# Order of three token tiles at the end of a hybrid decoder step

## The reference, cut to what matters

```python
x2 = LN2(alpha*x1 + HMoE(x1))   # top-1 group of experts, then top-2 experts in it
x3 = LN3(alpha*x2 + sigmoid(x2 @ w_ple_gate + b) * (p @ w_ple))
```

## Time and profile before

| what | value |
|---|---|
| median of three runs | 596.12 us |
| the profiled execution | 592.34 us |
| its span, first to last event | 590.7 us |
| TensorE busy | 535.6 us (91%) |
| VectorE busy | 293.3 us (50%) |
| ScalarE busy | 193.0 us (33%) |
| GpSimd busy | 58.0 us (10%) |

### The profile page before, as it was taken

The page is one execution under the profiler, slowest core; times in us unless marked ns, Lnnn a source line. Parts: engine busy times, 40 slices in busy tenths (PEclk is TensorE's granted clock), DMA queues, the critical chain, the costliest instruction groups (busy, mean ns, idle before and its releaser), DMA issues.

```text
span 590.7 us, 9533 instructions
## 1 busy us (share of the span) xinstructions
PE 535.6 (91%) x3628; PEld 385.0 (65%) x3628; DVE 293.3 (50%) x621; ACT 193.0 (33%) x363; POOL 58.0 (10%) x86
## 2 busy tenths in 40 slices
PE   4999789998999979999999999998888899888990
PEld 3999678887999978767664445444444445356870
DVE  3533786654475766686722322222222222378877
ACT  4444534443363360163141111111111121362532
POOL 2000003321352520000000000000000000000121
PEclk9999989999999999968999999999999999979996
DMA  8996237755232950195739999999999999940001
GB/s 277 370 348 216 88 117 210 252 199 165 81 131 58 326 206 1 50 426 236 275 135 423 421 421 424 420 424 421 423 420 424 419 424 417 363 184 1 1 36 53
DMA packets 47563, 151.86 MB, mean 257 GB/s; under 512 B 3104, under 2 KB 27877, under 8 KB 35104
## 3 DMA queue, kind: packets, MB, share of 16 engines
q1 hardware_dynamic: 42754, 136.93, 60.1%
q0 software_dynamic: 3728, 12.08, 6.4%
q10 hardware_dynamic: 1046, 2.37, 1.2%
HBM read 148.59 MB, written 2.90 MB: 256 GB/s over the span
## 4 chain that ended last, share of the span: by engine, by line
PE 72%; DMA 13%; DVE 9%; ACT 3%; issue 2%; SPq 0%; DVEq 0%; POOL 0%; POOLq 0%
PE bank L1482 16%; PE bank L1801 15%; DMA ring<-in_w_up_dram 11%; PE bank L1450 9%; PE bank L1814 7%; PE bank L1670 5%; PE bank L1823 2%; PE bank L1900 2%; PE bank L1748 2%; PE bank L1428 2%; PE bank L1537 1%; PE bank L1712 1%; PE bank L1702 1%; DMA arena<-in_x_prompt_dram 1%; PE bank L1807 1%
## 5 line engine op out<-in xcount | busy, mean ns | idle before, releaser
L1801 PE MATMUL bank<-ring,arena 128*64 128x256 f32 x1024 | 128.9, 392 | 10.6 <-DMA ring<-in_w_up_dram 7.3
L1801 PEld LDWEIGHTS bank<-ring,arena 128*64 128x64 f32 x1024 | 71.1, 134 | 66.6 <-issue 28.8
L1242 DVE TENSOR_TENSOR arena<-bank,arena 128x512 f32 x32 | 22.1, 692 | 143.7 <-PE bank L1823 143.7
L1482 PE MATMUL bank<-x_high,w_high 128*128 128x320 f32 x248 | 79.8, 322 | 0.0
L1482 PE MATMUL bank<-x_low,w_high 128*128 128x320 f32 x248 | 77.0, 311 | 0.0
L1482 PE MATMUL bank<-x_high,w_low 128*128 128x320 f32 x248 | 76.8, 310 | 0.0
L1814 PE MATMUL bank<-ring,arena 128*64 128x512 f32 x256 | 61.9, 604 | 0.0
L892 DVE TENSOR_TENSOR w_low<-ring,w_high 128x1024 fp32r<-128x1024 f32 x32 | 40.0, 1259 | 30.6 <-ACT w_high L573 30.6
L1482 PEld LDWEIGHTS bank<-x_high,w_high 128*128 128x128 f32 x248 | 47.2, 190 | 1.4 <-issue 1.3
L1482 PEld LDWEIGHTS bank<-x_low,w_high 128*128 128x128 f32 x248 | 47.2, 190 | 0.1
L1482 PEld LDWEIGHTS bank<-x_high,w_low 128*128 128x128 f32 x248 | 47.0, 189 | 0.0
(11 more groups left out here) (301 smaller groups left out, 881.9 us busy)
## 6 DMA issues: line engine op xcount, KB each, us to landing
ring<-in_w_gate_dram SPq DMA_DIRECT2D x32, 1024.0 KB, 18.0
ring<-in_w_up_dram SPq DMA_DIRECT2D x32, 1024.0 KB, 20.0
ring<-in_w_down_dram SPq DMA_DIRECT2D x32, 1024.0 KB, 16.7
ring<-in_w_in_dram SPq DMA_DIRECT2D x16, 1024.0 KB, 11.0
arena<-in_cache_k_dram POOLq DMA_DIRECT2D x16, 256.0 KB, 4.6
arena<-in_cache_v_dram POOLq DMA_DIRECT2D x16, 256.0 KB, 3.7
ring<-in_w_o_dram SPq DMA_DIRECT2D x4, 1024.0 KB, 9.6
ring<-in_w_ple_gate_dram SPq DMA_DIRECT2D x4, 1024.0 KB, 15.5
```

The source lines that it names most:

```text
L1242: V.tensor_tensor(YsT[:, :, bass.ds(place, WIN)].rearrange("p (d c) n -> p c d n", d=2), b[:, :].rearrange("p (c d n) -> p c d n", c=4, d= ...
L1482: last = mm(bank[j % 2][:, 0:T], w[:, j % 4, k, :], x[:, k, :], start=(k == n == 0), stop=(k == KD - 1 and n == 2))
L1801: last = mm(b[WIN * f:WIN * (f + 1), 0:256].rearrange("p (s n) -> p s n", s=2), x[:, WIN * k:WIN * (k + 1)], w[:, :, k, f, :], start=(k == ...
```

## The change

The tiles are taken in the order 0, 2, 1 from the sums on: `ORDER = (0, 2, 1)`, and the loops count places in this order. On every engine sums, norms, turns, gate products, residuals and stores follow it; banks and columns still belong to the tile. Tile 0 is turned behind the second of the five pieces of the last sum (now tile 1's). The fifth low part of the sorted results moves to the constants' space that the embedding weights have used, since x2_low of tile 0 is now written while that sum still reads it. On VectorE the last two `low_gate` pieces go behind `combined(3)`, one on either side of `low_columns(0)`; `norm3(0)` goes behind `low_columns` of the last tile; and `gates(5)` is no longer placed inside a norm.

```diff
-            (RING_AT + 4 * (UNIT * 10 + D), RING_AT + 4 * UNIT * 11, RING_AT + 4 * (UNIT * 11 + D), ARENA + 22528, ARENA + 88064))]
+            (RING_AT + 4 * (UNIT * 10 + D), RING_AT + 4 * UNIT * 11, RING_AT + 4 * (UNIT * 11 + D), ARENA + 22528, RING_AT + 4 * (UNIT * RING + C_PROMPT)))]
...
+        ORDER = (0, 2, 1)
...
-            for t in range(TILES):
-                sp.wait_ge(y_set, t + 1)
+            for place, t in enumerate(ORDER):
+                sp.wait_ge(y_set, place + 1)
...
             gate_out(0)
             norm(6)
             gate_out(1)
-            norm(7)
             high_columns(2)
             gate_out(2)
+            norm(7)
             gate_out(3)
             gate_out(4)
             norm(8)
...
             norm2(0)
-            for n in range(6, 8):
-                low_gate(n)
             combined(2)
             combined(3)
+            low_gate(6)
             low_columns(0)
+            low_gate(7)
             norm2(1)
             combined(4)
             combined(5)
...
             gates(0)
             low_columns(1)
             norm2(2)
             gates(1)
             residual(0)
-            norm3(0)
             gates(2)
             low_columns(2)
+            norm3(0)
             gates(3)
             residual(1)
             gates(4)
-            norm3(1, lambda: gates(5))
+            norm3(1)
+            gates(5)
             residual(2)
             norm3(2)
...
-            for t in range(1, TILES):
-                for n in range(5):
-                    combine(n, t)
-            turn_tile(x2, 0, x2t_ps, x2_set)
+            for n in range(5):
+                combine(n, ORDER[1])
+            for n in range(5):
+                if n == 2:
+                    turn_tile(x2, ORDER[0], x2t_ps, x2_set, 0)
+                combine(n, ORDER[2])
 
             for j in range(6):
-                t = j // 2
+                place = j // 2
+                t = ORDER[place]
                 if j in (1, 3):
-                    turn_tile(x2, (j + 1) // 2, x2t_ps, x2_set)
-                pe.wait_ge(x2t_a, 2 * t + 2)
-                pe.wait_ge(x2t_v, 2 * t + 2)
+                    turn_tile(x2, ORDER[place + 1], x2t_ps, x2_set, place + 1)
+                pe.wait_ge(x2t_a, 2 * place + 2)
+                pe.wait_ge(x2t_v, 2 * place + 2)
```

More of the change, by code:

```diff
@@ L545, in _ @@
             pool.wait_ge(pe_out, 6)
-            for t in range(TILES):
+            for place, t in enumerate(ORDER):
                 for hf in range(2):
-                    pool.wait_ge(pg_sig, 2 * t + hf + 1)
+                    pool.wait_ge(pg_sig, 2 * place + hf + 1)
                     v = gt[0:ROWS[t], t, 512 * hf:512 * (hf + 1)]
@@ L708, in norm @@
             def norm(n):
+                t = n - 1 if n <= TILES else ORDER[(n - 1) % TILES]
                 act.wait_ge(var_set, n)
-                v = rstd[0:ROWS[(n - 1) % TILES], (n - 1) % TILES:(n - 1) % TILES + 1]
+                v = rstd[0:ROWS[t], t:t + 1]
                 nc.scalar.activation(v, v, ACT.Sqrt).then_inc(sd_set, 1)
@@ L829, in _, with high_columns @@
             high_gate(7)
-            def high_columns(t):
+            def high_columns(place):
+                t = ORDER[place]
                 for g in range(2):
-                    act.wait_ge(x2t_ps, 2 * t + g + 1)
+                    act.wait_ge(x2t_ps, 2 * place + g + 1)
                     nc.scalar.copy(x2_high[:, 4 * g:4 * g + 4, P * t:P * t + ROWS[t]], four(bank[2 * t + g], ROWS[t])).then_inc(x2t_a, 1)
             def gate_out(n):
-                t, hf = n // 2, n % 2
+                t, hf = ORDER[n // 2], n % 2
                 act.wait_ge(pg_add, n + 1)
@@ L1078, in _, with layer_norm @@
             dve.wait_ge(x2_here, 32)
-            def layer_norm(x, t, gamma, beta, n, done, between=None):
+            def layer_norm(x, t, gamma, beta, n, done):
                 r = slice(0, ROWS[t])
@@ L1088, in layer_norm @@
                 link(V.scalar_tensor_tensor(v, v, mv[r, t, 0:1], gamma[r, :], ALU.subtract, ALU.mult))
-                if between:
-                    between()
                 dve.wait_ge(sd_set, n)
@@ L1339, in combined, with low_columns @@
                 dve.wait_ge(cm_ps, j + 1)
-                t, c = j // 2, half_of(j)
-                V.scalar_tensor_tensor(x2[0:ROWS[t], t, c], x1[0:ROWS[t], t, c], ALPHA, bank[j][0:ROWS[t], :], ALU.mult, ALU.add).then_inc(cm_used, 1)
-            def low_columns(t):
+                t, c = ORDER[j // 2], half_of(j)
+                V.scalar_tensor_tensor(x2[0:ROWS[t], t, c], x1[0:ROWS[t], t, c], ALPHA, bank[2 * t + j % 2][0:ROWS[t], :], ALU.mult, ALU.add).then_inc(cm_used, 1)
+            def low_columns(place):
+                t = ORDER[place]
                 for g in range(2):
-                    dve.wait_ge(x2t_a, 2 * t + g + 1)
+                    dve.wait_ge(x2t_a, 2 * place + g + 1)
                     c = slice(4 * g, 4 * g + 4)
@@ L1349, in low_columns, with norm2 @@
                     V.tensor_tensor(dst, four(bank[2 * t + g], ROWS[t]), x2_high[:, c, P * t:P * t + ROWS[t]].bitcast(F32), ALU.subtract).then_inc(x2t_v, 1)
-            def norm2(t):
-                dve.wait_ge(cm_used, 2 * t + 2)
-                layer_norm(x2, t, ln2[:, 0:D], ln2[:, D:2 * D], TILES + t + 1, x2_set)
+            def norm2(place):
+                dve.wait_ge(cm_used, 2 * place + 2)
+                layer_norm(x2, ORDER[place], ln2[:, 0:D], ln2[:, D:2 * D], TILES + place + 1, x2_set)
             for g in range(10):
@@ L1375, in gates @@
                 dve.wait_ge(pg_ps, j + 1)
-                t, c, b = j // 2, slice(512 * (j % 2), 512 * (j % 2 + 1)), bank[7 - j % 2]
+                t, c, b = ORDER[j // 2], slice(512 * (j % 2), 512 * (j % 2 + 1)), bank[7 - j % 2]
                 v = gt[0:ROWS[t], t, c]
@@ L1382, in gates, with residual @@
                 last.then_inc(pg_add, 1)
-            def residual(t):
+            def residual(place):
+                t = ORDER[place]
                 for hf in range(2):
-                    dve.wait_ge(pg_mul, 2 * t + hf + 1)
+                    dve.wait_ge(pg_mul, 2 * place + hf + 1)
                     v = x2[0:ROWS[t], t, 512 * hf:512 * (hf + 1)]
@@ L1390, in residual, with norm3 @@
                 link(last)
-            def norm3(t, between=None):
-                layer_norm(x2, t, ln3[:, 0:D], ln3[:, D:2 * D], 2 * TILES + t + 1, y_set, between)
+            def norm3(place):
+                layer_norm(x2, ORDER[place], ln3[:, 0:D], ln3[:, D:2 * D], 2 * TILES + place + 1, y_set)
             dve.wait_ge(cst_here, 80)
@@ L1418, in weights, with turn_tile @@
                 pe.wait_ge(w_in_slot[slot_of(i)], 16 * turn_of(i))
-            def turn_tile(src, t, ps, ready=None):
+            def turn_tile(src, t, ps, ready=None, place=None):
                 if ready:
-                    pe.wait_ge(ready, t + 1)
+                    pe.wait_ge(ready, (t if place is None else place) + 1)
                 r = ROWS[t]
@@ L1908, in _ @@
                 combine(n, 0)
-            for t in range(1, TILES):
-                for n in range(5):
-                    combine(n, t)
-            turn_tile(x2, 0, x2t_ps, x2_set)
+            for n in range(5):
[4 more added lines that the diff above has]
+                combine(n, ORDER[2])
             for j in range(6):
-                t = j // 2
+                place = j // 2
+                t = ORDER[place]
                 if j in (1, 3):
-                    turn_tile(x2, (j + 1) // 2, x2t_ps, x2_set)
-                pe.wait_ge(x2t_a, 2 * t + 2)
-                pe.wait_ge(x2t_v, 2 * t + 2)
+                    turn_tile(x2, ORDER[place + 1], x2t_ps, x2_set, place + 1)
+                pe.wait_ge(x2t_a, 2 * place + 2)
+                pe.wait_ge(x2t_v, 2 * place + 2)
                 if j >= 2:
                     pe.wait_ge(pg_add, j - 1)
-                by_parts(bank[7 - j % 2], j, lambda k, c0, c1: x2_high[:, k, c0:c1], lambda k, c0, c1: x2_low[:, k, c0:c1],
+                by_parts(bank[7 - j % 2], 2 * t + j % 2, lambda k, c0, c1: x2_high[:, k, c0:c1], lambda k, c0, c1: x2_low[:, k, c0:c1],
                          gw_high, gw_low, 4).then_inc(pg_ps, 1)
```

## The result

The changed kernel took 590.89 us (median of 14 runs) against 595.99 us for the kernel before in the same session. The ratio is 0.9939 with a 95% interval of 0.9912 to 0.9966: 3.6 us faster, between 2.0 and 5.2. The ratios here are taken from fast runs alone and are not the quotients of the medians beside them; the two medians lie 5.10 us apart, near the upper end of that interval. A second measurement (12 runs against 35) gave 0.9911 (0.9875 to 0.9948). The profiled execution took 589.49 us, its span is 587.8 us, the mean granted clock 0.975.

What follows compares the result with a forecast made beforehand. TensorE is busy almost throughout, but VectorE's chain behind the last products sets the end. 3.3 us from that chain (1.6 of it the turn) plus 0.3 from the store gave 3.6 less: 592.5 us, range 591.0 to 595.2.

Steps and rivals of the forecast that it cites:

- The turn: TensorE, inside the last sum: turn costs 0.90 us, hidden waits, so gate product 0 starts 1.58 us earlier.
- The rival in which the turn is not hidden: Tile 0's norm or low columns over 1 us late, product 0 still at 545.2; 2.0 us gained, 594.1; chance 0.14.
- The short tile's norm: VectorE, queued behind `low_gate(7)`: ready at 548.0, its turn on TensorE at 549.26, so 1.2 us spare.
- The slower rival: Short tile's norm late, TensorE idles before product 1, its clock falls; price 6.9 us, 599.4 in all; chance 0.04.
- The meeting of GpSimd's product with the last second norm: In `norm2(2)` GpSimd's product and a VectorE pass exclude each other: 0 to 1.29 us, taken as 1.0, hidden almost fully.
- a first pass near 2 us: Sign of being right: in the last second norm, VectorE's first pass takes near 2 us beside a GpSimd product.
- The meeting in `norm3(1)`: VectorE's third norm of tile 1 waits 0.4 us for a GpSimd product still running at its first pass.
- the rival with three of them: GpSimd products meet VectorE passes at more than two places, each up to 1.29 us; no gain left, 596; chance 0.06.
- VectorE's chain: From `gates(0)` to the last norm, VectorE sets the end: 583.97 against 587.29, 3.3 us earlier, 1.6 from the turn.
- The store: Last store, now 128 rows instead of 64: 2.07 against 2.38 us, 0.31 shorter; bounds -0.31 to 1.39.
- The rival by bytes: Last store costs by its bytes, 1.39 us more; 1.9 us gained, 594.2; chance 0.12.
- Nothing else moves: SyncE's queue, the moved low-part buffer and renumbered semaphores cost nothing.

Runs made afterwards that it cites:

- the late norm: Changed kernel with six extra statistics instructions on VectorE ahead of the short tile's norm; last norm ended 56.05 us from the sums' start, against 51.39.
- the experiment without the meeting: Changed kernel with GpSimd's first product held until the last second norm is done; last norm ended 51.37 us from the sums' start, against 51.39.
- the one with the turn behind the sums: Changed kernel with tile 0's turn put back behind the last sum, order 0, 2, 1 kept; 594.40 us, ratio 0.9987 to the kernel before.
- half the last store: Changed kernel storing only 64 of the last store's 128 rows; data moved until 2.27 us behind the issue, against 2.09.

## Why the prediction was right

The forecast was 3.6 us less, 592.5 on the median of 596.12, with a range of 591.0 to 595.2. From the sums' start to the end of the span the trace gave 3.98, and the timed ratio means 3.6 on the median of its session. On the median that the prediction started from, 0.9939 x 596.12 = 592.5. The absolute 590.89 lies 0.1 us below the low end of the range, less than the 0.55 by which the two measurements of the changed kernel differ, and the second ratio, 0.9911, would give 590.8. That forecast and first ratio meet at 3.6 is luck: the trace gives 3.98, the second ratio 5.3, and the intervals are over 3 us wide. What bears the prediction out is the edited stretch, term by term.

- **The turn.** Worked out: product 0 starts 1.58 us earlier. Measured: 1.70. The turn cost 0.87 in the chain, not 0.90. The slack of the low columns was 1.05 where 1.2 was worked out, that of tile 0's norm 0.92 (its pass ends at 540.00, the first transpose starts at 540.92) where 0.96 was. The rival in which the turn is not hidden fell.
- **The short tile's norm.** Slack worked out 1.2, measured 1.28, and by the experiment that took it away 1.29. The slower rival would have needed it 3.5 us late. Its price of 6.9 before the gain was too high, as the late norm showed.
- **The meeting of GpSimd's product with the last second norm.** Taken as 1.0. The second pass took 0.53 more; ahead of it VectorE waits 0.23 for ScalarE's square root, a wait that the sum did not have and that is not the meeting's, since it stands at 0.23 in the experiment without the meeting too. Both are hidden by product 2 as the text had it: VectorE still waits 0.20 for that product. Of the alternatives left open, the product waited first (2.40) and then the second pass (1.81). So one of the signs named for being right, a first pass near 2 us, did not come in the changed kernel; it came in the one with the turn behind the sums (2.03). The Trainium skill ("SBUF — State Buffer", the part on who interferes with whom) says that VectorE with two SBUF inputs and a GpSimd instruction that reads SBUF exclude each other, and that the second to issue blocks fully; 2.40 against 1.29 and the experiment's return to 1.28 and 1.29 agree with it, though both fall 0.1 to 0.2 short of a full block (554.73 - 553.48 + 1.29 = 2.54 and 555.88 - 555.15 + 1.28 = 2.01). The meeting in `norm3(1)` was taken as 0.4 and was 0.30 (1.58 less 1.28). No third meeting shows in the trace, and the rival with three of them fell.
- **VectorE's chain.** Worked out 3.3 us earlier at its end, measured 3.58: the turn gave 0.12 more, the chain behind it the rest.
- **The store.** Worked out 0.31 less by two rows of before; measured 2.09 against the old 2.38, 0.29 less, and 0.4 at the span's end. The rival by bytes fell, and half the store on the same tile showed it. The rule of the Trainium skill's "DMA: Bandwidth & Descriptors" (the anatomy of one DMA), a fixed part plus bytes, is fitted there to transfers that GpSimd issues, while SyncE issues these. It would have made the 64 rows quicker, by 0.60 us as an estimate with its figures; here they are 0.2 slower. The Trainium skill's "SBUF — State Buffer" has what fits (the section on the DMA port swizzle): 64 partitions reach half of the ports that 128 do, and it gives 196 against 328 GB/s for a larger transfer; here 188 to 229 stand against 410, the same direction.
- **What did not hold.** "Nothing else moves" is not contradicted for the change, but it did not hold for the executions. The sentence that the profile lay 3.8 us under the median "as a profile of one execution may" had a place to be found in: the stretch between the experts' end and the last sums was the shortest of ten in that profile, 14.50 where the others took 17.5 to 20.0. Setting the gain worked out in that profile against the median was right only because the edited stretch lies behind that place and repeats within 0.03 us.

## What to carry to other kernels

A step that feeds an engine's next stage can be put inside the last sum that does not need it, if what it waits for and what waits for it each have slack; work out both slacks in microseconds from the timeline before, since here the three slacks came out within 0.15 us. A run that takes one part of a change out keeps the others: here both kept the new list of VectorE, one edit of which costs 0.57 us in the old order, so the gains of two parts tested alone need not add up to the whole. Where run times scatter by more than the edit is worth, pick a mark just ahead of the edit and compare distances from it: they repeated within 0.03 us in kernels whose whole times differed by several.

## What was not expected of the hardware

- Behind the end of the experts TensorE stood still with no releaser that the trace names, and not for the same time: 2.57 us in the first trace of the changed kernel, 5.83 (2.2 of it ahead of the memset) and 1.70 in the second of the kernel before, 0.24 with three loads moved away. What it waits for there stays open.
- A store of 64 rows (256 KB) took longer than one of 128 (512 KB), 2.27 to 2.38 us against 2.07 to 2.09 from issue to the last data, in the traces of three kernels (before, changed, and, for 64 rows, half the last store), whether it was the last store or not.
- After 3.07 us without work TensorE's clock was granted at 0.50, but it rose again within the product that followed, so the fall cost 1.35 + 0.2 us and not a whole product at half speed.
